# Order of weight chunks, transposes and norms in the passages between eight layers

## Chip, cores and metric

One core of a Trainium2 chip runs the whole program. The metric is the time on the device in microseconds (us), the median of three runs; it says nothing of the host. All data is 32-bit float. TensorE works on pairs: each fp32 operand is split into a high part (written as fp32r) and the rest, and a product is made of three matmuls.

## What is computed

Eight layers over 512 tokens of 1024 numbers: gated linear attention, a spatial gating unit, forgetting attention, gated linear attention again, dilated attention with a memory, a feed-forward layer, a gated delta rule layer, a feed-forward layer. Around each of them stands the same frame, and the passage between two layers is the end of one frame and the start of the next:

```python
x = x + gate * rms_norm(o, norm_post_g[i])              # layers 0 to 3 (o = mixer(h) with w_out)
h = rms_norm(x, norm_pre_g[i]) * (1.0 + scale) + shift  # layers 0 to 3
x = x + _rms_norm(mixed, norm_mix_post[i])              # the layers behind them
h = _rms_norm(x, norm_ffn_pre[i])                       # and then h @ w_in of the next layer
```

## The kernel before

The tokens are four tiles of 128 (TT = 4), numbered t = 0 to 3. The program is written out engine by engine: each engine has one queue that it works off in order, and semaphores join them. For each of the seven passages with a layer on both sides, `trans_pe`, `trans_act` and `trans_dve` (L600, L716, L785) write the part of TensorE, ScalarE and VectorE. They are called in a row with the layers' own parts.

Weights come in chunks of 2 x 128 rows by up to 512 columns. SyncE loads them into a ring of NS = 6 slots (`sp_chunk`), and a slot is loaded again when TensorE has counted `w_used` up to the chunk that was in it. ScalarE copies a chunk to its high part (`act_feed`, L205), VectorE subtracts to the low part (`dve_feed`, L212), and TensorE waits for that (`w_lodone`). `f` is the first chunk of the next layer; its first block has the four chunks f to f+3.

In a passage each token tile goes through this chain:

- TensorE ends the output projection of tile t in PSUM banks 2t and 2t+1 (`out_half`, two halves of 512 columns).
- `squares(t)` on ScalarE (L726, L728): mean of squares of the output and its root.
- `post(t)` on VectorE (L795, L797, L801): reciprocal, times the gain, added to x.
- `xsquares(t)` on ScalarE (L736, L738): mean of squares of the new x and its root.
- `normed(t)` on VectorE (L805, L806): reciprocal, and x times it.
- `turn(t)` on TensorE (L627): eight transposes of 128 x 128 into the two banks of tile t.
- `spread(t)` on ScalarE (L745): eight activations with the scale (and, ahead of the layers 1 to 3, the shift) of the next norm.
- `split(t)` on VectorE (L812, L813): high and low part of the columns of hT that belong to tile t.

After that TensorE may multiply. `unit(u, c0, c1)` is a part of the first block of the next layer: unit u with the chunks f+c0 to f+c1-1. There are two forms of it. Ahead of layers 1, 2 and 3 (the token form) a unit is one token tile and needs `split(u)`; six matmuls of 512 columns for each chunk. Ahead of layers 4 to 7 (the halves form) a unit is 256 tokens and needs `split` of both its tiles; 24 matmuls of 256 columns for each chunk. In the halves form `unit(0, ...)` for the first two chunks is cut in two by `turn(2)`, and `turn(3)` stands ahead of `unit(0, 2, 4)`, which is the first to need the chunks f+2 and f+3. The first layer has no passage ahead of it (`cur` is None), and its own branches.

The waits that matter here are these: `unit` on `w_lodone` of its chunk and on `trans.sp` (split), `turn` on `trans.xn` (normed), `spread` on `trans.tr` (turn), `xsquares` on `x_done` (post), `squares(3)` on `w_used` of the last chunk of the old layer, `act_feed(f + 2)` and `act_feed(f + 3)` on their landing.

Of the kernel before, what the change touches and what calls it, by code (L numbers as in the profile page):

```python
# [59 lines left out]
def program(nc, io, out):  # L60
    ctx = ExitStack()
    with ctx:
# [133 lines left out]
        def width(n):  # L196
            return max(at + w for at, w, _ in chunks[n][0])

        def act_feed(upto):
            for n in range(fed.act, min(upto + 1, len(chunks))):  # L200
                m = width(n)
                nc.scalar.wait_ge(w_landed[n % NS], landed_at[n])
                if n >= NS:
                    nc.scalar.wait_ge(w_used, n - NS + 1)
                nc.scalar.activation(w_hi[:, n % NS, :, 0:m], w_raw[:, n % NS, :, 0:m], ACT.Copy).then_inc(w_hidone, 1)  # L205
            fed.act = max(fed.act, upto + 1)

        def dve_feed(upto):
            for n in range(fed.dve, min(upto + 1, len(chunks))):
                m = width(n)  # L210
                nc.vector.wait_ge(w_hidone, n + 1)
                nc.vector.tensor_tensor(w_lo[:, n % NS, :, 0:m], w_raw[:, n % NS, :, 0:m],  # L212
                                        w_hi[:, n % NS, :, 0:m].bitcast(F32), ALU.subtract).then_inc(w_lodone, 1)
            fed.dve = max(fed.dve, upto + 1)
# [385 lines left out]
        def trans_pe(cur, nxt, L):  # L600
# [23 lines left out]
            def turn(t):  # L624
                t_.wait_ge(trans.xn, n0 + t + 1)
                for k in range(KT):
                    mm = t_.transpose(PS[:, 2 * t + k // 4, (k % 4) * P:(k % 4 + 1) * P], nxt.xn[:, t, k * P:(k + 1) * P], ident[:])  # L627
                mm.then_inc(trans.tr, 1)
# [64 lines left out]
            if nxt.halves:  # L693
                unit(0, 0, 1, (0, 1))
                unit(0, 1, 2, (0, 1))
                turn(2)
                unit(0, 0, 1, (2, 3))
                unit(0, 1, 2, (2, 3))
                turn(3)
                unit(0, 2, 4)  # L700
                unit(1, 0, 4)
            else:
                unit(0, 0, 2)
                unit(1, 0, 2)
                if not cur:
                    t_.wait_ge(band_rows, 1)
                turn(2)
                unit(0, 2, 4)
                if not cur:
                    t_.wait_ge(modc_done, 1)  # L710
                turn(3)
                unit(1, 2, 4)
                unit(2, 0, 4)
                unit(3, 0, 4)

        def trans_act(cur, nxt, L):  # L716
            a = nc.scalar
            n0 = TT * L

            def squares(t):  # L720
                if t < TT - 1:
                    a.wait_ge(trans.out, (TT - 1) * (L - 1) + t + 1)
                else:
                    a.wait_ge(w_used, cur.ob.last + 1)
                junk = (nxt.xn if nxt else tail_junk)[:, t, :].rearrange("p (h c) -> p h c", h=2)
                then_act(a.activation(junk, PS[:, 2 * t:2 * t + 2, :], ACT.Square, scale=float(D) ** -0.5,  # L726
                                      accum_out=stat[:, 16 + t:17 + t]))
                a.activation(stat[:, 28 + t:29 + t], stat[:, 16 + t:17 + t], ACT.Sqrt, bias=eps[:]).then_inc(trans.sd, 1)  # L728

            def xsquares(t):  # L730
                if cur:
                    a.wait_ge(x_done, n0 - TT + t + 1)
                elif t == 0:
                    a.wait_ge(vcols_done, 1)
                    a.wait_ge(x_landed, 16)
                then_act(a.activation(nxt.xn[:, t, :], x[:, t, :], ACT.Square, scale=float(D) ** -0.5,  # L736
                                      accum_out=stat[:, t:t + 1]))
                a.activation(stat[:, 8 + t:9 + t], stat[:, t:t + 1], ACT.Sqrt, bias=eps[:]).then_inc(trans.sdx, 1)  # L738

            def spread(t):  # L740
                a.wait_ge(trans.tr, n0 + t + 1)
                if t == 0 and nxt.modulated:
                    a.wait_ge(*nxt.modulated)
                for k in range(KT):
                    ins = a.activation(nxt.xn[:, t, k * P:(k + 1) * P], PS[:, 2 * t + k // 4, (k % 4) * P:(k % 4 + 1) * P],  # L745
                                       ACT.Identity, scale=nxt.scale[:, k:k + 1],
                                       bias=nxt.bias[:, k:k + 1] if nxt.bias is not None else 0.0)
                ins.then_inc(trans.ev, 1)

            f = nxt.ins[0].first if nxt else None  # L750
            if not nxt:
                act_feed(cur.ob.last)
                for t in range(TT):
                    squares(t)
                return
            if not cur:
                for t in range(TT):
                    xsquares(t)
                act_setup()
                act_feed(f)  # L760
                spread(0)
                act_feed(f + 1)
                spread(1)
                act_bands()
                act_feed(f + 3)
                spread(2)
                spread(3)
                return
            act_feed(f + 1)
            squares(0)  # L770
            xsquares(0)
            squares(1)
            xsquares(1)
            spread(0)
            squares(2)
            spread(1)
            squares(3)
            xsquares(2)
            act_feed(f + 2)
            xsquares(3)  # L780
            act_feed(f + 3)
            spread(2)
            spread(3)

        def trans_dve(cur, nxt, L):  # L785
            v = nc.vector
            n0 = TT * L

            def post(t):
                n = n0 - TT + t  # L790
                y = (nxt.xn if nxt else tail_junk)[:, t, :]
                if t == 0:
                    v.wait_ge(*cur.g_ready)
                v.wait_ge(trans.sd, n + 1)
                then_dve(v.reciprocal(stat[:, 32 + t:33 + t], stat[:, 28 + t:29 + t]))  # L795
                for h in range(2):
                    ins = v.scalar_tensor_tensor(out=y[:, h * BW:(h + 1) * BW], in0=PS[:, 2 * t + h, :],  # L797
                                                 scalar=stat[:, 32 + t:33 + t], in1=cur.grow[:, h * BW:(h + 1) * BW],
                                                 op0=ALU.mult, op1=ALU.mult)
                then_dve(ins)  # L800
                v.tensor_tensor(x[:, t, :], x[:, t, :], y, ALU.add).then_inc(x_done, 1)  # L801

            def normed(t):
                v.wait_ge(trans.sdx, n0 + t + 1)
                then_dve(v.reciprocal(stat[:, 12 + t:13 + t], stat[:, 8 + t:9 + t]))  # L805
                v.tensor_scalar(nxt.xn[:, t, :], x[:, t, :], stat[:, 12 + t:13 + t], None, ALU.mult).then_inc(trans.xn, 1)  # L806

            def split(t):
                ts = slice(t * P, (t + 1) * P)
                v.wait_ge(trans.ev, n0 + t + 1)  # L810
                th = nxt.xn[:, t, :].rearrange("p (k s) -> p k s", s=P)
                then_dve(v.tensor_copy(hT_hi[:, :, ts], th))  # L812
                v.tensor_tensor(hT_lo[:, :, ts], th, hT_hi[:, :, ts].bitcast(F32), ALU.subtract).then_inc(trans.sp, 1)  # L813

            f = nxt.ins[0].first if nxt else None
            if not nxt:
                dve_feed(cur.ob.last)
                for t in range(TT):
                    post(t)
                return  # L820
            if not cur:
                for t in range(TT):
                    normed(t)
                dve_mod_first()
                dve_modfin(0, (7,))
                for t in range(TT):
                    dve_feed(f + (0, 1, 3, 3)[t])
                    split(t)
                return
            dve_feed(f + 1)  # L830
            post(0)
            normed(0)
            post(1)
            normed(1)
            split(0)
            post(2)
            split(1)
            normed(2)
            post(3)
            dve_feed(f + 2)  # L840
            normed(3)
            dve_feed(f + 3)
            split(2)
            split(3)

# [2454 lines left out]
```

## Time and profile before

| what | value |
|---|---|
| median of three runs | 2689.91 us (2689.34 to 2694.03) |
| the profiled execution | 2693.79 us, of which the traced span is 2692.1 us |
| TensorE matmul busy | 2546.3 us, 95% of the span |
| VectorE busy | 1375.1 us, 51% |
| ScalarE busy | 1090.2 us, 40% |
| GpSimd busy | 324.5 us, 12% |
| mean granted TensorE clock | 0.98 of full speed |

Busy time is a share of the span over stages that differ much from each other. TensorE is the engine that has work nearly all the time; the others have gaps. The places to read are those where TensorE sat idle, and by whom it was released: the profile's list of waits gives them by line, and the timeline of one passage shows what the engine did on both sides of such a gap. In the timeline a row's first number is its start, the second is how long it ran (in a merged row, all of its instructions together), and the brackets at its end hold the idle time ahead of it and what ended it. Where consecutive instructions of an engine overlap, the next one starts a little before the one ahead of it has ended.

### The profile page before, as it was taken

What the parts mean: (1) busy time and instruction counts of PE and PEld (TensorE: products, weight loads), DVE (VectorE), ACT (ScalarE), POOL (GpSimd) and SP (SyncE); (2) the same over time, 40 slices, a digit from 0 to 9 for tenths busy, and PEclk for the clock granted to TensorE, in tenths of its full rate; (3) what the DMA queues carried; (4) which work ended last, traced back from release to release, by engine and by line L of the source; (5) the groups of instructions that cost most, each with busy time, mean ns of one, the idle gap of its engine ahead of it and who ended that gap; (6) DMA issues with size and microseconds to landing.
All of it is one profiled execution on the core that took longest, in us unless ns stands there. A gap on an engine that the chain in (4) does not pass through costs nothing.

```text
span 2692.1 us, 32843 instructions
## 1 busy us (share of the span) xinstructions
PE 2546.3 (95%) x12894; PEld 2090.8 (78%) x12894; DVE 1375.1 (51%) x2343; ACT 1090.2 (40%) x1878; POOL 324.5 (12%) x519
## 2 busy tenths in 40 slices
PE   4989999999999999999999999999998999999998
PEld 3777778778766778788967888888786898888887
DVE  5678576557464556653234533324577554533322
ACT  4455342343353555454363422214544454522221
POOL 2233011011200013110000000001014330000000
PEclk9999999999999999999999999999999999999999
DMA  6522265346310421143201333333322210333332
GB/s 225 196 75 87 89 228 179 93 137 190 122 36 27 128 87 53 42 137 88 70 1 32 110 94 102 95 94 111 107 73 61 64 33 15 104 94 99 97 94 78
DMA packets 159713, 258.79 MB, mean 96 GB/s; under 512 B 24911, under 2 KB 77930, under 8 KB 158537
## 3 DMA queue, kind: packets, MB, share of 16 engines
q1 hardware_dynamic: 140544, 202.54, 24.4%
q0 software_dynamic: 16768, 52.50, 5.9%
q8 instruction: 103, 1.69, 0.3%
q10 hardware_dynamic: 2249, 1.65, 0.2%
q14 instruction: 49, 0.40, 0.1%
HBM read 249.78 MB, written 10.02 MB: 97 GB/s over the span
## 4 chain that ended last, share of the span: by engine, by line
PE 51%; DVE 4%; ACT 4%; DMA 1%; issue 1%; POOL 1%; SPq 0%; DVEq 0%; ACTq 0%
PE PS L220 13%; PE PS L221 13%; PE PS L222 13%; PE PS L1821 2%; PE PS L1837 1%; PE PS L980 1%; PE PS L2517 1%; DVE x L801 1%; PE PS L1828 1%; POOL dn_zero L2418 1%; PE PS L2508 1%; PE PS L2534 0%; DVE dn_qkvT L2964 0%; PE PS L2571 0%; PE PS L2471 0%
## 5 line engine op out<-in xcount | busy, mean ns | idle before, releaser
L212 DVE TENSOR_TENSOR w_lo<-w_raw,w_hi 128x1024 fp32r<-128x1024 f32 (+1 forms) x348 | 413.7, 1198 | 739.5 <-ACT w_hi L205 738.3
L205 ACT ACTIVATE w_hi<-w_raw 128x1024 fp32r<-128x1024 f32 (+1 forms) x348 | 357.7, 1035 | 1051.0 <-DMA w_raw<-in_ffn_w_gate_up 309.2
L220 PE MATMUL PS<-hT_hi,w_hi 128*128 128x512 f32 (+1 forms) x1600 | 608.1, 380 | 16.9 <-DVE hT_lo L813 12.4
L222 PE MATMUL PS<-hT_hi,w_lo 128*128 128x512 f32 (+1 forms) x1600 | 600.1, 375 | 0.0
L221 PE MATMUL PS<-hT_lo,w_hi 128*128 128x512 f32 (+1 forms) x1600 | 599.9, 375 | 0.0
L220 PE MATMUL PS<-w_hi,hT_hi 128*128 128x512 f32 (+1 forms) x864 | 347.8, 403 | 24.7 <-ACT gla_szT L1057 8.7
L220 PEld LDWEIGHTS PS<-hT_hi,w_hi 128*128 128x128 f32 x1600 | 305.3, 191 | 74.3 <-issue 17.5
L222 PEld LDWEIGHTS PS<-hT_hi,w_lo 128*128 128x128 f32 x1600 | 304.4, 190 | 53.4
L221 PEld LDWEIGHTS PS<-hT_lo,w_hi 128*128 128x128 f32 x1600 | 305.1, 191 | 51.0 <-issue 0.2
L221 PE MATMUL PS<-w_lo,hT_hi 128*128 128x512 f32 (+1 forms) x864 | 339.2, 393 | 0.0
L222 PE MATMUL PS<-w_hi,hT_lo 128*128 128x512 f32 (+1 forms) x864 | 338.8, 392 | 0.0
L220 PEld LDWEIGHTS PS<-w_hi,hT_hi 128*128 128x128 f32 x864 | 175.4, 203 | 62.0 <-issue 12.3
L222 PEld LDWEIGHTS PS<-w_hi,hT_lo 128*128 128x128 f32 x864 | 174.8, 202 | 32.1
L221 PEld LDWEIGHTS PS<-w_lo,hT_hi 128*128 128x128 f32 x864 | 175.1, 203 | 30.4 <-issue 1.3
L463 POOL DMA_DIRECT2D mraw<-in_w_mod x160 | 86.3, 540 | 472.5 <-DVE macc L512 469.7
L512 DVE SCALAR_TENSOR_TENSOR macc<-mraw,cond,macc 128x512 f32<-128x512 f32 x160 | 121.8, 761 | 35.2 <-DMA mraw<-in_w_mod 32.3
L221 PE MATMUL PS<-w_lo,ffn_hi 128*128 128x512 f32 x352 | 138.8, 394 | 0.0
L220 PE MATMUL PS<-w_hi,ffn_hi 128*128 128x512 f32 x352 | 138.2, 393 | 0.0
L222 PE MATMUL PS<-w_hi,ffn_lo 128*128 128x512 f32 x352 | 136.8, 389 | 0.0
L220 PEld LDWEIGHTS PS<-w_hi,ffn_hi 128*128 128x128 f32 x352 | 66.1, 188 | 15.4
L222 PEld LDWEIGHTS PS<-w_hi,ffn_lo 128*128 128x128 f32 x352 | 66.1, 188 | 14.7
L221 PEld LDWEIGHTS PS<-w_lo,ffn_hi 128*128 128x128 f32 x352 | 66.3, 188 | 13.1
(639 smaller groups left out, 3407.9 us busy)
## 6 DMA issues: line engine op xcount, KB each, us to landing
w_raw<-in_ffn_w_gate_up SPq DMA_DIRECT2D x176, 256.0 KB, 3.2
mraw<-in_w_mod POOLq DMA_DIRECT2D x160, 256.0 KB, 4.0
w_raw<-in_gla_w_in SPq DMA_DIRECT2D x48, 512.0 KB, 4.8
w_raw<-in_ffn_w_down SPq DMA_DIRECT2D x44, 512.0 KB, 3.8
w_raw<-in_fox_w_in SPq DMA_DIRECT2D x32, 512.0 KB, 3.8
w_raw<-in_sgu_w_in SPq DMA_DIRECT2D x24, 512.0 KB, 4.5
w_raw<-in_dn_w_in SPq DMA_DIRECT2D x24, 512.0 KB, 3.7
w_raw<-in_gla_w_out SPq DMA_DIRECT2D x16, 512.0 KB, 4.6
```

Source lines behind the costliest of these rows:

```text
L205: nc.scalar.activation(w_hi[:, n % NS, :, 0:m], w_raw[:, n % NS, :, 0:m], ACT.Copy).then_inc(w_hidone, 1)
L212: nc.vector.tensor_tensor(w_lo[:, n % NS, :, 0:m], w_raw[:, n % NS, :, 0:m], w_hi[:, n % NS, :, 0:m].bitcast(F32), ALU.subtract).then_inc( ...
L220: nc.tensor.matmul(o, l_hi, r_hi, start=start, stop=False)
L221: nc.tensor.matmul(o, l_hi, r_lo, start=False, stop=False)
L222: return nc.tensor.matmul(o, l_lo, r_hi, start=False, stop=stop)
L463: eng.dma_start(mraw[:, n % MS, 0, :], w[:, i % KT, m * BW:(m + 1) * BW]).then_inc(p_landed[n % MS], 16)
L512: nc.vector.scalar_tensor_tensor(out=acc, in0=mraw[:, n % MS, 0, :], scalar=cond[:, i % KT:i % KT + 1], in1=acc, op0=ALU.mult, op1=ALU.add ...
L801: v.tensor_tensor(x[:, t, :], x[:, t, :], y, ALU.add).then_inc(x_done, 1)
L980: mm = pe_.matmul(PS[:, l % 2, ts], a, m, start=True, stop=True)
L1821: t_.matmul(PS[:, w.u % 3, 0:w.n], w.q, w.k, start=True, stop=True).then_inc(su.sc, 1)
L1828: mm = t_.transpose(PS[:, 3 + w.u % 2, k * P:(k + 1) * P], Pb[:, w.u % 3, k * P:(k + 1) * P], ident[:])
L1837: mm = t_.matmul(PS[w.rows, 5 + w.pair % 2, w.t * P:(w.t + 1) * P], w.v[k], PT[:, w.u % 2, k * P:(k + 1) * P], start=k == 0, stop=k == nk - 1)
```

## The change

Three orders are changed; no instruction is added or taken away.

- TensorE, token form, with a layer ahead: `unit(0, 2, 4)` moves from behind `turn(2)` to ahead of it, and `unit(1, 2, 4)` from behind `turn(3)` to ahead of it. The halves form keeps its order. The first layer keeps its own.
- ScalarE, all seven passages: `act_feed(f + 2)` moves ahead of `squares(3)`; `act_feed(f + 3)` stays behind `xsquares(2)` and ahead of `spread(2)`, and `xsquares(3)` moves from ahead of `act_feed(f + 3)` to behind `spread(2)`.
- VectorE, all seven passages: `dve_feed(f + 2)` moves ahead of `normed(2)`, and `dve_feed(f + 3)` ahead of `post(3)`.

```diff
@@ -704,12 +704,16 @@
                 unit(1, 0, 2)
                 if not cur:
                     t_.wait_ge(band_rows, 1)
+                unit(0, 2, 4) if cur else None
                 turn(2)
-                unit(0, 2, 4)
                 if not cur:
                     t_.wait_ge(modc_done, 1)
+                    unit(0, 2, 4)
+                else:
+                    unit(1, 2, 4)
                 turn(3)
-                unit(1, 2, 4)
+                if not cur:
+                    unit(1, 2, 4)
                 unit(2, 0, 4)
                 unit(3, 0, 4)
 
@@ -774,12 +778,12 @@
             spread(0)
             squares(2)
             spread(1)
+            act_feed(f + 2)
             squares(3)
             xsquares(2)
-            act_feed(f + 2)
-            xsquares(3)
             act_feed(f + 3)
             spread(2)
+            xsquares(3)
             spread(3)
 
         def trans_dve(cur, nxt, L):
@@ -835,11 +839,11 @@
             split(0)
             post(2)
             split(1)
+            dve_feed(f + 2)
             normed(2)
+            dve_feed(f + 3)
             post(3)
-            dve_feed(f + 2)
             normed(3)
-            dve_feed(f + 3)
             split(2)
             split(3)
```

## Rows read from the trace of the kernel before

**Rows 1.** Waits of PE, whole span: us in total, times, longest

```profile
PE PS L220 <- DVE hT_lo L813: 16.7, 8, 3.3
...
PE PS L220 <- DVE w_lo L212: 6.1, 6, 1.1
```

**Rows 2.** Timeline of PE, passage into layer 1: start, duration, idle before

```profile
332.61 0.47 PE L220 MATMUL PS<-w_hi,hT_hi 128*128 128x512 f32 x1 [1.35 <-DVE hT_lo L813]
...
335.45 1.04 PE L627 MATMUL PS<-ident,sgu0x_xn 128*128 128x128 f32 x8
337.60 0.50 PE L220 MATMUL PS<-w_hi,hT_hi 128*128 128x512 f32 x1 [1.11 <-DVE w_lo L212]
...
340.18 0.50 PE L220 MATMUL PS<-w_hi,hT_hi 128*128 128x512 f32 x1 [0.92 <-DVE w_lo L212]
...
341.68 1.04 PE L627 MATMUL PS<-ident,sgu0x_xn 128*128 128x128 f32 x8
342.47 0.48 PE L220 MATMUL PS<-w_hi,hT_hi 128*128 128x512 f32 x1
```

**Rows 3.** Timeline of ACT, passage into layer 1

```profile
329.81 1.06 ACT L726 ACTIVATE sgu0x_xn<-PS 128x1024 f32<-128x1024 f32 x1
...
331.19 1.04 ACT L736 ACTIVATE sgu0x_xn<-x 128x1024 f32<-128x1024 f32 x1
...
332.55 1.04 ACT L205 ACTIVATE w_hi<-w_raw 128x1024 fp32r<-128x1024 f32 x1
336.44 1.06 ACT L736 ACTIVATE sgu0x_xn<-x 128x1024 f32<-128x1024 f32 x1 [2.85 <-DVE x L801]
...
337.63 0.29 ACT L738 ACTIVATE stat<-stat,eps 128x1 f32<-128x1 f32 x1
337.83 1.04 ACT L205 ACTIVATE w_hi<-w_raw 128x1024 fp32r<-128x1024 f32 x1
338.77 2.88 ACT L745 ACTIVATE sgu0x_xn<-PS,modc 128x128 f32<-128x128 f32 x8
```

**Rows 4.** Timeline of DVE, passage into layer 1

```profile
333.55 0.16 DVE L795 RECIPROCAL stat<-stat 128x1 f32<-128x1 f32 x1
...
336.33 1.22 DVE L212 TENSOR_TENSOR w_lo<-w_raw,w_hi 128x1024 fp32r<-128x1024 f32 x1
337.95 0.16 DVE L805 RECIPROCAL stat<-stat 128x1 f32<-128x1 f32 x1 [0.41 <-ACT stat L738]
338.15 0.76 DVE L806 TENSOR_SCALAR sgu0x_xn<-x,stat 128x1024 f32<-128x1024 f32 x1
...
341.68 0.69 DVE L812 CAST hT_hi<-sgu0x_xn 128x1024 fp32r<-128x1024 f32 x1 [1.55 <-ACT sgu0x_xn L745]
342.41 1.22 DVE L813 TENSOR_TENSOR hT_lo<-sgu0x_xn,hT_hi 128x1024 fp32r<-128x1024 f32 x1
```

**Rows 5.** DMA issues, 1171 to 1180 us: count, KB, median us to landing

```profile
w_raw<-in_att_w_in SPq DMA_DIRECT2D x4, 512.0 KB, 4.8
```

**Rows 6.** Timeline of PE, passage into layer 4 (halves form)

```profile
1180.22 0.55 PE L220 MATMUL PS<-hT_hi,w_hi 128*128 128x256 f32 x1 [3.33 <-DVE hT_lo L813]
...
1184.66 1.03 PE L627 MATMUL PS<-ident,attx_xn 128*128 128x128 f32 x8
...
1188.40 1.03 PE L627 MATMUL PS<-ident,attx_xn 128*128 128x128 f32 x8
```

**Rows 7.** Timeline of ACT, passage into layer 4

```profile
1186.08 2.15 ACT L745 ACTIVATE attx_xn<-PS,vcols 128x128 f32<-128x128 f32 x8
```

**Rows 8.** Timeline of PE, passage into layer 7

```profile
2321.06 0.35 PE L220 MATMUL PS<-hT_hi,w_hi 128*128 128x256 f32 x1 [2.43 <-DVE hT_lo L813]
2324.01 1.03 PE L627 MATMUL PS<-ident,ffn1x_xn 128*128 128x128 f32 x8
...
2327.80 1.09 PE L627 MATMUL PS<-ident,ffn1x_xn 128*128 128x128 f32 x8
```

**Rows 9.** Busy time by stretch: us, PE, PEld, DVE, ACT, POOL, PEclk, DMA

```profile
1180.20:1183.60 3.40, 3.38 (x16) 3.40 (x17) 3.33 (x5) 0.48 (x1) 0.00 (x0) 0.50 0.10 39
```

## Prediction

> **What bounds the kernel now.** TensorE has work for nearly the whole span, so I looked first at the list of its waits [rows 1]. Two lines of it lie in the passages. The wait for the low part of hT, 16.7 us in 8 cases, is mostly the wait for `split(1)`; the wait for a weight chunk's low part, 6.1 us in 6 cases, is two waits in each of the three passages of the token form. No `turn` waits long. Then I read one passage of each form on TensorE. Token form [rows 2]: behind `split(1)` 1.35 us idle, `unit(1, 0, 2)` at 332.61, `turn(2)` at 335.45, then 1.11 and 0.92 us idle for the chunks f+2 and f+3, `turn(3)` at 341.68, `unit(1, 2, 4)` at 342.47. The other two token passages have the same pattern. Halves form [rows 6]: 3.33 us idle behind `split(1)`, `turn(2)` at 1184.66, `turn(3)` at 1188.40, and nothing idle between or behind. So a passage is bound by TensorE except where a chain through ScalarE and VectorE ends later than its matmuls. The change can gain only the two chunk waits of the token form: 3 x 2.03 = 6.1 us. The halves form has no chunk wait to remove.
>
> **Part 1, chunks f+2 and f+3 earlier (ScalarE, VectorE).** On ScalarE `act_feed(f + 2)` takes the place of `squares(3)` at 329.81 [rows 3]. A feed takes 0.94 us to the next start (337.83 to 338.77), so `squares(3)` starts at 330.75, `xsquares(2)` 1.38 later (329.81 to 331.19 in the old order) at 332.13, and `act_feed(f + 3)` 1.36 later (331.19 to 332.55) at 333.5, ended 334.5. On VectorE the low part of f+2 goes behind `split(1)`, which ends just before TensorE's start at 332.61; at 1.22 us [rows 4] it is there by 333.7. `normed(2)` follows, then the low part of f+3, from 334.55 to 335.8. TensorE wants f+2 at 335.45 and f+3 at some 336.8. Both chunk waits go. The feeds cost nothing of their own: both engines pay the same two instructions earlier. If f+2 lands late, `squares(3)` and all behind it on ScalarE wait with it. In the halves passage the load is issued when its slot comes free, and lands 4.8 us later [rows 5]; ScalarE is ready for it about then (1171.9 + 4.8 = 1176.7). I take 0: by the starts above `normed(2)` ends at 333.5 + 0.04 + 0.96 = 334.5 in the token passage, and `turn(2)` isn't due before 338.2 (Part 2), so a landing later by less than some 3 us costs nothing there.
>
> **Part 2, `turn(2)` later (token form).** `unit(0, 2, 4)`, 12 matmuls, now stands ahead of it. Twelve matmuls of this size took 335.45 - 332.61 = 2.84 us with their start. `turn(2)` moves from 335.45 to 338.2 and ends 1.04 later at 339.2. These matmuls aren't extra work; what matters is who waits for `turn(2)`.
>
> **Part 3, `xsquares(3)` behind `spread(2)` (all seven).** This is where I find the cost. In the old order `xsquares(3)` ran at 336.44, as soon as `post(3)` was done, and `normed(3)` was ready at 338.9, long before `turn(3)` [rows 2 to 4]. In the new order the third tile's whole chain stands between `turn(2)` and `turn(3)`. From the end of `turn(2)`: `spread(2)` 2.75 us (2.88 less the overlap of some 0.13 with the next instruction), `xsquares(3)` with its root 1.48 (336.44 to 337.63 + 0.29), `normed(3)` 0.96 (337.95 to 338.15 + 0.76), handovers 0.15: 5.3 us. So `turn(3)` starts at 339.2 + 5.3 = 344.5. Meanwhile TensorE has only `unit(1, 2, 4)`, 2.8 us, till 341.8. A new wait of 2.7 us stands ahead of `turn(3)`. Behind it on VectorE `split(2)` must now wait for `normed(3)`, since they share a queue: 344.5 + 1.95 (341.68 to 342.41 + 1.22) = 346.4, and `unit(2, 0, 4)` starts at 346.5, after a second new wait of about 1 us. In the old order it started at 342.47 + 2.8 = 345.25. The passage ends later by 1.25, say 1.3 us; the removed 2.03 us are already inside this difference. Three passages: 3.9 us.
>
> In the halves form `turn(2)` stays where it is, and TensorE has two parts of `unit(0, ...)` between the turns. `turn(2)` ends at 1184.66 + 1.03 = 1185.69 [rows 6]. `spread(2)` is shorter here, 2.15 [rows 7], 2.0 to the next start; with 1.48, 0.96 and handovers the chain takes 4.55 us, and `turn(3)` starts at 1190.25 in place of 1188.40: later by 1.85 us. `post(3)` isn't late for it: in the token passage it took 2.78 us (333.55 to 336.33) [rows 4] and is moved by two feeds of 1.22, so it ends by 338.6, against `xsquares(3)` at 342.0; in the halves passage `xsquares(3)` can't start before 1187.7. Behind `turn(3)` TensorE has the 48 matmuls of `unit(0, 2, 4)`, some 5.8 us, and `spread(3)` and `split(3)` take 2.15 + 1.95 from its end, so nothing waits again. The passages into the layers 5 and 6 have the same distance between the turns. Into layer 7: 2324.01 + 1.03 + 4.55 = 2329.6 in place of 2327.80 [rows 8], 1.8 us. Together 3 x 1.85 + 1.8 = 7.35 us.
>
> All of this lies on TensorE's path, and every other engine of the next layer is fed by TensorE's output, so I carry it to the end one to one. Sum of waits: 3.9 + 7.35 = 11.25 us.
>
> **Part 4, the clock.** After the idle 3.33 us in the passage into layer 4 the granted clock was 0.50, the level of 1.2 GHz, for 3.4 us [rows 9]. The 24 matmuls from there to `turn(2)` took 4.44 us, where the same 24 took 2.95 in the passage into layer 7 after an idle 2.43 us [rows 6, 8]; so the price was 1.5 us, and not every wait pays it. The new token waits of 2.7 us, with another of 1 us close behind, lie between these two. Bounds for each: 0, or 1.5 us where the slow stretch falls on matmuls; less where it falls on a wait that is there anyway. I take 0.6 for each, an estimate nearer to the lower row: 1.9 us. The new halves waits of some 1.7 us are below the row that paid nothing; I take 0.
>
> The Trainium skill, page "TensorE: Matmul & The Clock Gate", section "Why this matters for your kernels", says that throughput drops mid-kernel are avoided by leaving no long idle gaps between bursts of matmuls, since the clock then falls back. The trace agrees for the 3.33 us gap, and by that rule joining short waits into one long one is the wrong direction, which is what this change does ahead of `turn(3)`; were each of the three token waits to pay the whole 1.5 us, the sum would be 11.25 + 4.5 = 15.75 us.
>
> **Sum.** 11.25 + 1.9 = 13.1 us. The profiled execution's own time is 2693.79 us, its span 2692.1; this would give 2706.9 for such an execution. It was near the top of the three runs shown, 3.9 us above the median, and the median is what is compared: 2689.9 + 13.1 = 2703.0 us.
>
> **Rivals.**
> - *The half clock follows the new waits widely.* All three token waits pay 1.5 us, and the halves waits, each followed by eight short transposes, pay too: 11.25 + 4.5 + 4 x 1.5 = 21.75, 2711.7 us. For it: waits of 3.3 us pay. Against: 2.43 us did not [rows 8]. A chance of 0.08.
> - *The time is given back.* Later in each layer TensorE waits for something that doesn't depend on the passage (a load, a chain on VectorE), and that swallows the delay; it decides from 6 us swallowed on. Price: all of 11.25 given back is 2690, half of it 2695. For it: TensorE does wait in the mixers. Against: what releases it there is computed from the projections that come late themselves, and in the feed-forward layers nothing waits. A chance of 0.08 that no more than 5.4 us is left, and none below.
> - *The chain hides, and only the gain is left.* If `xsquares(3)` were ready before TensorE has done its 2.8 us, the result would be the removed waits alone: 2689.9 - 6.1 = 2683.8 us. It needs the chain between the turns to be under 2.8 us in the token form, and under 2.7 in the halves form; the rows make it 5.3 and 4.55. Only a mistake of mine on the order of the queues would allow it. A chance of 0.04.
>
> **How the numbers follow.** My forecast of new waits ahead of `turn(3)`, little or partly slowed by the clock, has 0.80, with its own range 2697 to 2709. The low side takes 0 for the clock (2701.2) and some us swallowed or a base lower by the spread of the runs; the high side takes all token waits at 1.5 us (2705.7) and some of the halves waits. The range on record, 2695 to 2711, reaches to the half-absorbed case and almost to the wide half clock. The measurement can tell some 0.2%, 5.4 us, from no change. Slower by more than that: 0.80 + 0.08 = 0.88. Within: 0.08. Faster: 0.04.
>
> **What would show it.** In the trace of after, the chunk waits (`w_lo`, L212) are gone from the list for TensorE, 6.1 us in 6 cases to about 0. In their place stands a wait of L627 on `normed` (L806): some 2.7 us in each token passage and 1.7 to 1.9 us in each halves passage, near 15 us in 7 cases. The wait for `split` (L813) grows by about 1 us in each token passage. `xsquares(3)` starts where `spread(2)` ends, with no idle time ahead of it. If `turn(3)` doesn't wait, part 3 is wrong; if it does and the total is unmoved, the delay was swallowed, and later waits must be shorter than before. If `squares(3)` starts late after an idle stretch that a load ended, part 1 is wrong. Granted clock 0.5 behind `turn(3)` decides part 4.

## Result and profile after

The changed kernel is slower. Beside the kernel before it took 2713.62 us (median of 4 runs, 2710.12 to 2716.71) against 2690.41 us (4 runs, 2689.34 to 2694.03): a ratio of 1.0071, 95% interval 1.0049 to 1.0093. Measured again beside 32 runs of the kernel before it took 2710.88 us (9 runs) against 2697.06: 1.0068, interval 1.0045 to 1.0090. The prediction was 2703.0 us with a range of 2695 to 2711, and a move of 13.1 us. The direction was right, the place too, the size was too small: the move is 18 us (0.0068 x 2697) to 23 us. In absolute time the first median lies 2.6 us above the range; by the ratio on the prediction's own base (1.0071 x 2689.9 = 2709.0 us) it lies inside, near the upper end.

One thing about the base matters for every number below. In the longer comparisons the kernel before took 2687.35 to 2711.06 us over 35 runs, median 2696.61, and 2680.66 to 2704.46 over 32 runs. The first runs, on which the prediction's 2689.9 rests, lay in the lower part of that. Ratios are therefore taken within one comparison only.

The page of the profiled execution of after (2710.12 us, its span 2708.4):

```profile
span 2708.4 us, 32842 instructions
...
PE 2553.3 (94%) x12894; PEld 2092.9 (77%) x12894; DVE 1375.5 (51%) x2343; ACT 1090.6 (40%) x1878; POOL 324.0 (12%) x519
```

The work is the same, 12894 matmuls; only the span grew. The waits of PE over the whole span of after (us in total, times, longest) stand against [rows 1]:

```profile
PE PS L220 <- DVE hT_lo L817: 19.2, 11, 3.3
...
PE PS L627 <- DVE fox0x_xn L810: 2.8, 2, 2.6
...
PE PS L627 <- DVE sgu0x_xn L810: 2.6, 1, 2.6
PE PS L627 <- DVE gla1x_xn L810: 2.6, 1, 2.6
...
PE PS L627 <- DVE ffn0x_xn L810: 1.8, 1, 1.8
PE PS L627 <- DVE dnx_xn L810: 1.8, 1, 1.8
PE PS L627 <- DVE attx_xn L810: 1.7, 1, 1.7
PE PS L627 <- DVE ffn1x_xn L810: 1.7, 1, 1.7
```

The line of waits for a chunk's low part, 6.1 us in 6 cases before, is gone. In its place each of the seven passages has a wait of `turn(3)` (L627) for `normed(3)`: 2.59 us in the token form, 1.75 us in the halves form, 14.8 us in seven passages. The wait for `split` has grown from 16.7 us in 8 cases to 19.2 in 11: three more, one in each token passage.

The timeline of PE in the passage into layer 1 of after, against [rows 2]:

```profile
331.12 0.47 PE L220 MATMUL PS<-w_hi,hT_hi 128*128 128x512 f32 x1 [1.34 <-DVE hT_lo L817]
...
336.69 1.04 PE L627 MATMUL PS<-ident,sgu0x_xn 128*128 128x128 f32 x8
337.48 0.48 PE L220 MATMUL PS<-w_hi,hT_hi 128*128 128x512 f32 x1
...
343.07 1.09 PE L627 MATMUL PS<-ident,sgu0x_xn 128*128 128x128 f32 x8 [2.59 <-DVE sgu0x_xn L810]
...
345.02 0.77 PE L220 MATMUL PS<-w_hi,hT_hi 128*128 128x512 f32 x1 [0.86 <-DVE hT_lo L817]
```

And that of ACT in the same passage, against [rows 3]:

```profile
328.31 1.10 ACT L205 ACTIVATE w_hi<-w_raw 128x1024 fp32r<-128x1024 f32 x1
329.26 1.06 ACT L730 ACTIVATE sgu0x_xn<-PS 128x1024 f32<-128x1024 f32 x1
...
337.77 2.90 ACT L749 ACTIVATE sgu0x_xn<-PS,modc 128x128 f32<-128x128 f32 x8 [4.70 <-PE PS L627]
340.52 1.09 ACT L740 ACTIVATE sgu0x_xn<-x 128x1024 f32<-128x1024 f32 x1
...
344.20 2.90 ACT L749 ACTIVATE sgu0x_xn<-PS,modc 128x128 f32<-128x128 f32 x8 [2.17 <-PE PS L627]
```

VectorE ended `post(3)` in the same passage with this row:

```profile
335.88 1.23 DVE L805 TENSOR_TENSOR x<-x,sgu0x_xn 128x1024 f32<-128x1024 f32 x1
```

ScalarE sits idle for 4.70 us until `turn(2)` comes. Then `spread(2)` (337.77) and `xsquares(3)` (340.52, L740) stand in a row, although `post(3)` on VectorE had been done at 335.88 + 1.23 = 337.1. `xsquares(3)` could have started then, in the last 0.7 us of the idle time and ahead of `spread(2)`; its place in the queue forbade it, and it started 3.4 us later. From the end of `turn(2)` (337.73) to `turn(3)` (343.07) it is 5.34 us; the prediction had 5.3.

To separate passages from the rest, I took from the start of each matmul the length of every passage: from the first transpose of `turn(0)` over 164 matmuls and transposes in the token form, 260 in the halves form (with a kernel's added matmuls on top), which is the same work in each kernel. In brackets how long the granted clock was at half in it. Worked out from the traces' starts, one profiled execution each, in us:

```
                into layer:  1           2           3           4           5           6           7           sum
before                       37.83 (0)   37.87 (0)   37.85 (0)   39.85 (3.4) 39.86 (3.4) 39.60 (3.4) 37.49 (0)   270.3
after                        40.68 (3.4) 41.98 (6.8) 40.74 (3.4) 43.10 (6.8) 41.79 (3.4) 41.72 (3.4) 39.34 (0)   289.4
after, again                 39.12 (0)   41.20 (6.8) 40.41 (3.4) 43.09 (6.8) 41.78 (3.4) 41.71 (3.4) 40.84 (3.4) 288.2
e1 turns back                38.06 (0)   38.07 (0)   39.70 (3.4) 41.66 (3.4) 41.86 (3.4) 41.79 (3.4) 40.85 (3.4) 282.0
e2 norm back                 37.68 (0)   37.67 (0)   39.29 (3.4) 41.08 (6.8) 40.07 (3.4) 40.05 (0)   39.44 (0)   275.3
e3 fill                      39.16 (0)   39.14 (0)   39.14 (0)   41.78 (3.4) 41.82 (3.4) 41.83 (3.4) 41.12 (3.4) 284.0
e4 shorter                   35.45 (0)   35.48 (0)   35.45 (0)   38.26 (0)   38.29 (0)   38.30 (0)   38.20 (0)   259.4
e5 units only                40.43 (0)   40.44 (0)   40.40 (0)   41.10 (6.8) 39.85 (3.4) 38.35 (0)   38.91 (3.4) 279.5
e6 before, filled            37.82 (0)   37.85 (0)   37.83 (0)   38.36 (0)   38.35 (0)   38.36 (0)   37.49 (0)   266.1
e7 token only                40.76 (3.4) 40.69 (3.4) 40.47 (3.4) 39.75 (3.4) 39.86 (3.4) 41.07 (6.8) 37.49 (0)   280.1
```

The passages of after are 19.1 and 17.9 us longer in its two traces. Outside of them before has 2421.7 us, after 2419.0 and 2426.7: the loss is in the passages. Outside of them all ten traces lie between 2415.8 and 2428.1, with no order by kernel; that spread alone is as large as some of the effects looked for, so a few us given back there could not be seen.

### The profile page after: what moved, and what is told of

The parts are those of the page before. It is cut to its first block, busy times and chain, and to the rows that moved or that the text cites. A ratio compares the mean times of both kernels' runs of the same rounds, so it can differ in the third digit from the quotient of the medians.

```text
span 2708.4 us, 32842 instructions
## 1 busy us (share of the span) xinstructions
PE 2553.3 (94%) x12894; PEld 2092.9 (77%) x12894; DVE 1375.5 (51%) x2343; ACT 1090.6 (40%) x1878; POOL 324.0 (12%) x519
## 4 chain that ended last, share of the span: by engine, by line
PE 51%; DVE 5%; ACT 4%; DMA 1%; issue 1%; POOL 1%; SPq 0%; DVEq 0%; ACTq 0%
PE PS L220 13%; PE PS L221 13%; PE PS L222 13%; PE PS L1825 2%; PE PS L1841 1%; PE PS L984 1%; PE PS L2521 1%; DVE x L805 1%; PE PS L1832 1%; POOL dn_zero L2422 1%; PE PS L2512 1%; PE PS L2538 0%; DVE dn_qkvT L2968 0%; PE PS L2575 0%; PE PS L2475 0%
## 5 line engine op out<-in xcount | busy, mean ns | idle before, releaser
L220 PE MATMUL PS<-hT_hi,w_hi 128*128 128x512 f32 (+1 forms) x1600 | 608.2, 380 | 16.5 <-DVE hT_lo L817 12.4
L222 PEld LDWEIGHTS PS<-w_hi,ffn_lo 128*128 128x128 f32 x352 | 66.1, 188 | 14.8
L221 PEld LDWEIGHTS PS<-w_lo,ffn_hi 128*128 128x128 f32 x352 | 66.2, 188 | 13.1
```

The costliest lines, as they stand in the source:

```text
L220: nc.tensor.matmul(o, l_hi, r_hi, start=start, stop=False)
L221: nc.tensor.matmul(o, l_hi, r_lo, start=False, stop=False)
L222: return nc.tensor.matmul(o, l_lo, r_hi, start=False, stop=stop)
```

## Experiments

Theory W: the time follows the new waits of TensorE, one to one. Theory C: the waits, and the half clock that follows the long ones, which costs about as much again in the token passages.

**e1, the turns back.** The changed kernel with TensorE's order of before.

```diff
-                unit(0, 2, 4) if cur else None
                 turn(2)
+                unit(0, 2, 4)
                 if not cur:
                     t_.wait_ge(modc_done, 1)
-                    unit(0, 2, 4)
-                else:
-                    unit(1, 2, 4)
                 turn(3)
-                if not cur:
-                    unit(1, 2, 4)
+                unit(1, 2, 4)
```

> The changed kernel, with TensorE's order of before in the token form (each turn again ahead of the second half of its unit). Theory W (the time is the sum of TensorE's new waits): turn(2) comes 2.75 us earlier, and the chain behind it with it, so in a token passage the chunk waits are gone, one wait of about 2.6 us stands ahead of turn(3), none behind it, and the passage ends within 0.2 us of before; the four halves passages keep their 1.75 us. Sum 3 x 0.1 + 7.4 = 7.7, time 2698. Theory C (waits, and half clock behind them in the token passages, some 10 us in all): the 2.6 us waits are still there, so most of that stays: 2704 to 2709.

Measured: ratio 1.0041 (1.0023 to 1.0059), 2709.78 against 2696.61 us. PE in the passage into layer 1:

```profile
335.16 1.04 PE L627 MATMUL PS<-ident,sgu0x_xn 128*128 128x128 f32 x8
...
341.54 1.09 PE L627 MATMUL PS<-ident,sgu0x_xn 128*128 128x128 f32 x8 [2.59 <-DVE sgu0x_xn L806]
```

The wait of 2.59 us comes whether `turn(2)` is early or late: it is the chain behind `turn(2)`, less the 2.8 us of matmuls between the turns. With `turn(2)` early the two passages without half clock are 0.2 us longer than before. So moving TensorE's units cost the token passage 1.1 us (39.12 - 38.06), and the reordered norm used up what the removed chunk waits had given. The total of 11 us lies between the theories' 7.7 and 14 to 19 on this base; half clock came in one token passage of three, behind a wait of 2.59 us with no second one near it, and the total can't decide.

**e2, the norm back.** The changed kernel with one line moved.

```diff
             act_feed(f + 3)
-            spread(2)
             xsquares(3)
+            spread(2)
             spread(3)
```

> The changed kernel, with xsquares(3) ahead of spread(2) again (behind act_feed(f+3)), nothing else. Both theories: no wait ahead of turn(3) in the token form, but one of about 2.4 us ahead of unit(2, 0, 4), since turn(2) is still late; the token passage ends as before. In the halves form the wait ahead of turn(3) falls from 1.75 us to 0.3 or less. Theory W: waits sum to +1 us, time 2691 to 2692. Theory C: up to 1.5 us more for each of the three token waits, 2692 to 2697. If the loss lay in the earlier feeds (they are all kept here), the time would stay at 2713.

Measured: ratio 1.0009 (0.9993 to 1.0025). With the early feeds kept, moving this one line takes the ratio from 1.0068 to 1.0009, some 16 us. PE in the passage into layer 1:

```profile
336.17 1.04 PE L627 MATMUL PS<-ident,sgu0x_xn 128*128 128x128 f32 x8
339.79 1.04 PE L627 MATMUL PS<-ident,sgu0x_xn 128*128 128x128 f32 x8
...
343.03 0.47 PE L220 MATMUL PS<-w_hi,hT_hi 128*128 128x512 f32 x1 [2.20 <-DVE hT_lo L817]
```

`turn(3)` waits for nothing; the idle time is in one piece behind it, 2.20 us for `split(2)`, and the passage is as long as before (37.68 us; into layer 3 a stretch of half clock followed that wait, 39.29 us). The early chunks gain nothing, since the third tile, whose turn is late, is the next thing that TensorE lacks. Against this run, `spread(2)` starts 0.76 us sooner behind the start of `turn(2)` in after (337.77 - 336.69 against 338.01 - 336.17), and `xsquares(3)` 3.4 us later (340.52 against 336.62).

In the halves passages the expectation, 0.3 us or less ahead of `turn(3)`, holds into layers 4 and 5 and fails into layers 6 and 7, where 1.47 and 1.76 us are left. PE, ACT and DVE in the passage into layer 7:

```profile
2327.40 1.23 DVE L805 TENSOR_TENSOR x<-x,ffn1x_xn 128x1024 f32<-128x1024 f32 x1
2328.66 1.06 ACT L740 ACTIVATE ffn1x_xn<-x 128x1024 f32<-128x1024 f32 x1 [4.07 <-DVE x L805]
...
2331.17 1.09 PE L627 MATMUL PS<-ident,ffn1x_xn 128*128 128x128 f32 x8 [1.76 <-DVE ffn1x_xn L810]
```

Here `xsquares(3)` waits for `post(3)`, and `post(3)` stands behind both early `dve_feed`s on VectorE. From the passage's start `xsquares(3)` comes at 18.72 us (2328.66 - 2309.94), where the kernel before has 16.77 (2325.28 - 2308.51), and the passage is 1.95 us longer. Into layer 6 it is 1.7 us longer than in e5, which has before's order on ScalarE and VectorE and no half clock there either. Into layers 4 and 5 TensorE was held up by half clock ahead of `turn(2)` and needed tile 3 later. So the early feeds are not free in the halves form: in these two passages they alone make `turn(3)` late. In after the later `xsquares(3)` hides this.

**e3, the wait filled.** The changed kernel with matmuls into a bank that `turn(3)` overwrites, ten in the token form and seven in the halves form; nobody reads them.

```diff
+            def fill(m):
+                if cur:
+                    t_.wait_ge(x_done, n0)
+                    w = w_hi[:, b.first % NS, 0, :]
+                    for _ in range(m):
+                        t_.matmul(PS[:, 6, :], w[:, 0:P], w, start=True, stop=True)
...
+                fill(7)       # halves; fill(10) in the token form
                 turn(3)
```

> The changed kernel, with matmuls whose results nobody reads in the wait ahead of turn(3): ten of 512 columns in the token form, seven in the halves form, into bank 6, which turn(3) overwrites. They take 2.3 and 1.6 us, a little less than the waits of 2.59 and 1.75 us, so turn(3) starts when it did; only TensorE isn't idle in between. Theory C: no half clock follows, the waits alone are left, 2690.4 + 11.2 = 2701.6 (2699 to 2704). Theory W (the clock has no part in the difference): 2713, as the changed kernel.

Measured: ratio 1.0030 (1.0014 to 1.0046), where the same kernel without them has 1.0068. PE in the passage into layer 1:

```profile
335.27 1.04 PE L627 MATMUL PS<-ident,sgu0x_xn 128*128 128x128 f32 x8
...
338.90 2.43 PE L677 MATMUL PS<-w_hi 128*128 128x512 f32 x10
341.65 1.09 PE L627 MATMUL PS<-ident,sgu0x_xn 128*128 128x128 f32 x8 [0.33 <-DVE sgu0x_xn L819]
...
343.60 0.47 PE L220 MATMUL PS<-w_hi,hT_hi 128*128 128x512 f32 x1 [0.86 <-DVE hT_lo L826]
```

From the start of `turn(2)` to that of `turn(3)` it is 6.38 us in both (335.27 to 341.65, and 336.69 to 343.07 without the filling), so the waits weren't shortened. Yet the passages are 39.14, 39.14 and 39.16 us long, with no half clock in any, against 40.68, 41.98 and 40.74 in one trace of after and 39.12 (no half clock), 41.20 and 40.41 in the other. That is theory C: useless work in a wait saves time, since what is left are the bare waits, 1.3 us a passage as predicted. The ratio's 8 us is even a little below the 11.5 us of waits (interval 3.8 to 12.4 us, which just touches that of after). In the halves passages the filling gained nothing that shows: the half clock there follows the old wait for `split(1)`, which was not filled, and into layers 5 and 6 the passages are as long as in after (41.82 and 41.83 us against 41.79 and 41.72).

**e7, the token passages alone.** The changed kernel with ScalarE's and VectorE's order of before where `nxt.halves` holds (the edit in short form).

```diff
+            if nxt.halves:
+                squares(3); xsquares(2); act_feed(f + 2); xsquares(3)
+                act_feed(f + 3); spread(2); spread(3)
+                return
             act_feed(f + 2)
             squares(3)
...
+            if nxt.halves:
+                normed(2); post(3); dve_feed(f + 2); normed(3)
+                dve_feed(f + 3); split(2); split(3)
+                return
             dve_feed(f + 2)
             normed(2)
```

> The changed kernel with ScalarE's and VectorE's order of before in the four halves passages; the three token passages are changed. Theory W: the halves passages' 7.35 us are gone, 3.9 us are left, ratio 1.0014. Theory C: the half clock behind the three token waits stays, up to 1.5 us each, ratio 1.0022 to 1.0031.

Measured: ratio 1.0038 (1.0019 to 1.0057), some 10 us, above both theories' figures. PE in the passage into layer 1; behind the second wait the first matmul ran 0.76 us, where it is 0.47 to 0.48 at full clock:

```profile
345.12 1.09 PE L627 MATMUL PS<-ident,sgu0x_xn 128*128 128x128 f32 x8 [2.59 <-DVE sgu0x_xn L819]
...
347.07 0.76 PE L220 MATMUL PS<-w_hi,hT_hi 128*128 128x512 f32 x1 [0.86 <-DVE hT_lo L826]
```

All three token passages had half clock, and each is 2.6 to 2.9 us longer than before: 1.3 for the waits and as much again for the clock, 8.4 us in three. Theory W has 3.9 for them.

**e5, TensorE's part alone.** The kernel before with only the first hunk of the change.

> The kernel before with TensorE's part of the change alone (each turn behind the second half of its unit, in the token form). Both theories: the chunks f+2 and f+3 are prepared as late as before, so the wait for f+2 grows to about 2.1 us, that for f+3 stays near 1.1 us, and unit(2, 0, 4) waits some 1.6 us for split(2), as turn(2) and spread(2) come later. No wait ahead of turn(3). The token passage ends 2.5 us later than before, the halves passages as before: 7.6 us in all, ratio 1.0028, some more by theory C (up to 1.0040).

Measured: ratio 1.0035 (1.0014 to 1.0055), passages into layers 1 to 3 2.6 us longer (2.5 expected), all without half clock. PE in the passage into layer 1:

```profile
335.36 0.50 PE L220 MATMUL PS<-w_hi,hT_hi 128*128 128x512 f32 x1 [2.03 <-DVE w_lo L212]
...
337.95 0.50 PE L220 MATMUL PS<-w_hi,hT_hi 128*128 128x512 f32 x1 [0.93 <-DVE w_lo L212]
339.46 1.04 PE L627 MATMUL PS<-ident,sgu0x_xn 128*128 128x128 f32 x8
...
345.57 0.47 PE L220 MATMUL PS<-w_hi,hT_hi 128*128 128x512 f32 x1 [1.42 <-DVE hT_lo L817]
```

A unit moved ahead of a turn only moves the idle time ahead of the turn too, and everything behind the turn gets it. The three waits, 2.03, 0.93 and 1.42 us, are more idle time than the 2.59 + 0.86 us of after, but in pieces, and no half clock followed in any of the three passages.

**e6, the old wait filled.** The kernel before, with nine such matmuls in the wait for `split(1)` of the halves passages.

```diff
             if nxt.halves:
+                t_.wait_ge(w_lodone, b.first + 1)
+                fill(9)       # here behind trans.sp of tile 0, into bank 0
                 unit(0, 0, 1, (0, 1))
```

> The kernel before with nine matmuls of 512 columns, whose results nobody reads, in the wait for split(1) of each halves passage. They take 2.0 us of the 3.33 us (of 2.43 in the passage into layer 7), so unit(0) starts when it did. Theory C: the half clock behind the 3.33 us waits goes, and with it 1.5 us in each of three passages: ratio 0.9983. Theory W (half clock costs nothing that shows in the whole): 1.0000.

Measured: ratio 0.9988 (0.9972 to 1.0005). The whole can't tell it from no change. The trace can: the passages into layers 4 to 6 are 38.36, 38.35 and 38.36 us long, against 39.85, 39.86 and 39.60, with no half clock where there were 3.4 us in each. PE in the passage into layer 4, against [rows 6]:

```profile
1181.14 0.36 PE L220 MATMUL PS<-hT_hi,w_hi 128*128 128x256 f32 x1 [1.30 <-DVE hT_lo L822]
1184.09 1.03 PE L627 MATMUL PS<-ident,attx_xn 128*128 128x128 f32 x8
```

From the first matmul to `turn(2)` it is 2.95 us in place of 4.44. The price of 1.5 us for a stretch of half clock on matmuls, on which the prediction's bound rests, holds.

**e4, a shorter order.** The same operations, ordered by the durations of the trace so that TensorE waits least (the edit in short form; the first layer keeps its own order).

```diff
 # TensorE, token form
-unit(0,0,2); unit(1,0,2); turn(2); unit(0,2,4); turn(3); unit(1,2,4)
+unit(0,0,2); unit(0,2,3); turn(2); unit(0,3,4); unit(1,0,4); turn(3)
 # ScalarE, token form
-squares(2); spread(1); squares(3); xsquares(2); act_feed(f+2); xsquares(3); act_feed(f+3); spread(2); spread(3)
+squares(2); spread(1); act_feed(f+2); xsquares(2); act_feed(f+3); squares(3); spread(2); xsquares(3); spread(3)
 # VectorE, token form
-post(2); split(1); normed(2); post(3); dve_feed(f+2); normed(3); dve_feed(f+3); split(2); split(3)
+post(2); dve_feed(f+2); normed(2); dve_feed(f+3); split(1); post(3); split(2); normed(3); split(3)
 # ScalarE, halves form
+spread(1); squares(2); act_feed(f+2); squares(3); act_feed(f+3); xsquares(2); xsquares(3); spread(2); spread(3)
 # VectorE, halves form
+split(1); post(2); post(3); normed(2); normed(3); dve_feed(f+3); split(2); split(3)
 # TensorE, halves form: both turns behind unit(0, 0, 1, ...) and unit(0, 1, 2, ...)
```

> Orders made from the durations of the trace so that TensorE waits least. Token form, TensorE: unit 0 with f, f+1, f+2, then turn(2), unit 0 with f+3, unit 1 whole, turn(3); ScalarE: squares(2), spread(1), feed f+2, xsquares(2), feed f+3, squares(3), spread(2), xsquares(3), spread(3); VectorE: post(2), lo f+2, normed(2), lo f+3, split(1), post(3), split(2), normed(3), split(3). Halves form: spread(1) and split(1) ahead of squares(2) and post(2), feeds on ScalarE early, all of unit(0, 0, 2) ahead of turn(2) and turn(3). Token: waits of about 0.9, 0.1 and 0.5 us in place of 1.35, 1.11 and 0.92, the passage 2.4 us shorter than before. Halves: 1.6, 0.6, 0.8 and 0.3 us in place of 3.33 us, as long as before by the waits, and 1.5 us shorter where the half clock followed the 3.33 us. Theory W: 2690.4 - 7.2 = 2683. Theory C: 3 x 1.5 less, 2679.

Measured: ratio 0.9959 (0.9942 to 0.9976), 2688.34 against 2696.61 us in medians (12 runs): the fastest of all, and clear of both other kernels. PE in the passages into layer 1 and layer 4:

```profile
329.49 0.50 PE L220 MATMUL PS<-w_hi,hT_hi 128*128 128x512 f32 x1 [0.96 <-DVE w_lo L212]
...
330.99 1.03 PE L627 MATMUL PS<-ident,sgu0x_xn 128*128 128x128 f32 x8
...
333.75 0.47 PE L220 MATMUL PS<-w_hi,hT_hi 128*128 128x512 f32 x1 [0.30 <-DVE hT_lo L830]
...
1171.04 0.36 PE L220 MATMUL PS<-hT_hi,w_hi 128*128 128x256 f32 x1 [1.61 <-DVE hT_lo L830]
...
1177.36 1.09 PE L627 MATMUL PS<-ident,attx_xn 128*128 128x128 f32 x8 [0.35 <-DVE attx_xn L823]
...
1179.00 1.09 PE L627 MATMUL PS<-ident,attx_xn 128*128 128x128 f32 x8 [0.54 <-DVE attx_xn L823]
```

Token passages are 2.4 us shorter than before, as expected. Here `turn(2)` comes early, and unit 1 as a whole (24 matmuls) stands between the turns, which covers the chain. The waits of the halves passages are 1.61, 0.35 and 0.54 us in place of one of 3.33 us; no half clock follows, and the passages are 1.3 to 1.6 us shorter. Into layer 7, where the old wait paid no half clock, the order is 0.7 us worse. Passages: 10.9 us in all, against 11 us (0.0041 x 2697) in the whole.

The changed kernel itself, run again:

> The changed kernel as it is, beside the kernel before in many runs, since single runs of the kernel before spread over 2687 to 2711 us. Theory W (waits alone, 11.2 us): ratio 1.0042. Theory C (waits, and half clock behind the token waits of 2.59 us): 1.0050 to 1.0065.

Measured: 1.0068 (1.0045 to 1.0090), above theory C's 1.0050 to 1.0065 by a hair and consistent with it; 1.0042 lies just outside the interval.

## Why the prediction was right or wrong

- *What bounds the kernel, and the gain of 6.1 us.* Right for this change: the chunk waits are gone from the list, and nothing else was gained. Another order could gain more, as e4 shows (10.9 us in the passages).
- *Part 1, the feeds.* Right: no load held ScalarE up, `squares(3)` started at 329.26 with the feed ahead of it at 328.31, 0.95 us. That the feeds cost nothing of their own holds only behind the late `xsquares(3)`: into layer 7 of after `post(3)` ended at 2341.3 and `xsquares(3)` started at 2341.6. Where that is taken back (e2), the two feeds ahead of `post(3)` cost 1.7 and 1.95 us in the passages into layers 6 and 7.
- *Part 2.* Right: `turn(2)` came 336.69 - 331.12 = 5.57 us behind the first matmul of `unit(1, 0, 2)`, where [rows 2] have 2.84; 2.73 later, and with e1 one sees that this costs 1.1 us a passage.
- *Part 3, the chain between the turns.* Right in mechanism and size for the order as changed. Wait ahead of `turn(3)`: 2.59 and 1.75 us, predicted 2.7 and 1.7; second wait 0.86, predicted 1. Net for a token passage without half clock 1.29 us (39.12 - 37.83), predicted 1.3; for the halves passages 1.93 and 1.92 (into layer 5) and 2.12 (layer 6), predicted 1.85; into layer 7 1.85, predicted 1.8. The sum of waits is 11.5 to 12 us, predicted 11.25. Nothing given back shows outside of the passages, to within their spread of 12 us.
- *Part 4, the clock.* This is the step that failed in size: the term was 1.9 us. In nine token passages with the wait of 2.59 us ahead of `turn(3)` and the late `turn(2)` (after twice, e7), there were ten stretches of half clock of 3.4 us, twice two in a row, once none; the mean length is 40.67 us against 39.14 with the wait filled, 1.5 us each and 4.6 us in three. I had placed the 2.6 us wait between a row at 2.43 us that paid nothing [rows 8] and one at 3.33 that paid [rows 6, 9], and took the lower. But the lower row was one draw: the same wait into layer 7, 2.40 to 2.70 us in the eight traces that have it unchanged, was followed by half clock in four of them (after again, e1, e3, e5). The estimate of 15.75 us, with the whole price for each token wait, was the better forecast. The rule of the Trainium skill that stood beside it (page "TensorE: Matmul & The Clock Gate", section "Why this matters for your kernels") speaks of longer gaps than 2.59 us; its direction is borne out, its gap is not, since the clock fell here after shorter ones too. The second wait of 0.86 us close behind the first may be why the clock fell so often: e1 has the first wait alone and half clock in one token passage of three, against eight of nine. Three passages are few, and the two weren't tried apart on purpose.
- *What remains.* 11.5 + 4.6 = 16 us, against 18 us measured with an interval of 12 to 24. The half clock that two traces of after show twice in a row into layer 4, and one into layer 7, is no effect of the change that could be shown: e5, whose halves passages are as before, has both (41.10 and 38.91 us). A single trace of the kernel before, 3.4 us in each of three passages and none in the fourth, wasn't a safe picture of the clock there.
- *The base.* The other part of the miss in absolute time. Three runs gave 2689.9; 67 runs give 2697. The range should have held that spread, and it took the three runs' 5 us for it.
- *Rivals.* The gain alone (2683.8) is excluded by the traces, and so is the time given back as far as the 6 us that it needed: the ratio's lower end is 12 us, above the 11.25 us of waits. The wide half clock (2711.7) came near in number, through the token passages and not through the halves passages that it needed.

## What to carry to other kernels

Before an operation is moved behind another in an in-order queue, ask what the other one waits for: `xsquares(3)` needed only `post(3)`, and behind `spread(2)` it also needed `turn(2)`; `spread(2)` started 0.76 us sooner for it and `xsquares(3)` 3.4 us later. Ask it on every engine: `post(3)` behind two feeds was late in the halves form too, and one late chain hid the other until e2 took the first away. A wait removed from the bounding engine is worth only the distance to the next chain that it lacks, and the order has to be costed from that chain, between the two turns here. Idle time in short pieces was cheaper here than in one, as the fall of the clock comes on top (e5: 4.4 us in three pieces, no half clock in three passages; after and e7: 3.45 us, 2.59 of it in one, half clock in eight of nine); where one long wait can't be avoided, work that nobody reads may pay for itself.

## What was not expected of the hardware

- Matmuls without use made the whole faster: 2.43 us of them in a wait of 2.59 us gave 39.14 to 39.16 us for the passage, where it took 40.4 to 42.0 us in eight of nine without them (39.12 in the ninth).
- A stretch of half clock may be followed by a second one with TensorE busy. Busy time by stretch in after, passage into layer 2 (columns as in [rows 9]):

```profile
549.30:551.80 2.50, 0.00 (x0) 0.00 (x0) 0.91 (x3) 1.49 (x4) 0.00 (x0) 1.00 0.00 0
553.04:559.87 6.83, 6.05 (x14) 4.84 (x15) 4.51 (x7) 4.74 (x10) 0.00 (x0) 0.50 0.01 0
```

The idle stretch ran at full granted clock; 1.2 us behind it the clock went to half for 6.8 us, in which TensorE was busy for 6.05: it was idle for the first 0.78 us, the rest of the second wait, and not after that. That passage is 4.1 us longer than before.
- One kernel's time spread over 24 us in 35 runs (2687.35 to 2711.06), 0.9%; with twelve runs beside some thirty the intervals are still 0.3% to 0.4% wide, and e2 and e6 stay undecided in the whole while their passages are clear in the trace.
